# Second MLP of a two-block transformer kernel: unit 1 computed with seven block products instead of two plain columns, and the steps around it moved

## The chip, the core and the metric

One core of a Trainium2 chip runs the whole program. TensorE (PE in the profile) multiplies, ScalarE (ACT) and VectorE (DVE) prepare operands and take results out of the accumulators, GpSimd (POOL) and SyncE (SP) issue the DMAs. The metric is the device time of one execution in microseconds (us), as a median over runs.

## What is computed

Two blocks run one after the other on 256 tokens of width 2048. The change touches only the MLP at the end of the second block:

```python
h2 = rmsnorm(x, g_mlp[l])
u = jax.nn.relu(jnp.einsum('bsd,df->bsf', h2, w_up[l]))
x = x + jnp.einsum('bsf,fd->bsd', u * u, w_down[l])
...
return rmsnorm(x, g_final)
```

`w_up` is 2048 x 8192 and `w_down` 8192 x 2048, both float32: 64 MB each, read from HBM once.

## The kernel before

**Precision.** Every float32 operand is split into a high part and a low part (what the high part leaves). A product takes three matmuls: high x high, high x low of the weights, low x high. They are L626, L627 and L628 in plain products and L656, L657 and L658 (helper `three`) in the block products described below. ACT writes the high part of the weights into `w_high`, DVE then subtracts it from `raw` and writes `w_low`. In plain stretches these are L1154 and L1671, around block products and everything behind them L1283 and L1874. Both rings have four places (`LEAD = 4`). A filling of one place is called a *piece* here; `half_used` counts the pieces that PE has finished, and ACT may write piece n+4 only once PE is through with piece n.

**Units.** The hidden width is worked through in eight units of 1024. A unit has an up product (h2 by `w_up`, 16 pieces of plain work or 24 of block work), a squared ReLU, a redistribution, and a down product (16 pieces, `fast_down`) that adds to `xs`. A plain piece feeds 12 matmuls. A unit done with seven block products (`fast_up`) goes through four pairs of weight loads. Of the first load of a pair (`seven_products`) come pieces of 6, 6, 6 and 3 matmuls, of the second (`eight_products`) two pieces of 12: 45 matmuls a pair, 180 a unit. The seven products need sums of weight blocks, which DVE makes right behind the low part of a pair's first piece (`sum_weights`: L1888, L1891, L1893, all of which the second and third piece of the pair need), and sums of token blocks, called `combos`, made once for the whole MLP: eight DVE adds (`sum_tokens`, L1905 to L1913), one ACT copy (`split_combos`, L1294), one DVE subtraction (`low_combos`, L1918). The seven products that come out are put together by eight DVE adds (`combine`, L1926).

**The hidden half between up and down.** For every column of 512: ReLU on ACT (L1364 from PSUM behind plain work, L1311 behind block work), square on ACT (L1370 or L1316), block transposes on DVE (`turn_blocks`, L1988), sixteen DMAs that exchange 32-row blocks (from `blocks` in `scr` to `exchanged` in `extra`), high part on ACT (`take_exchanged`, L1225) and low part on DVE (`take_low`, L1865) into `u_high` and `u_low`. There is one `exchanged` buffer: the transposes of a column stand behind the take of the column before on DVE.

**Order.** Nothing schedules at run time. Each engine has a list written by hand, and semaphores tie the lists. In `first_eighths` ACT and DVE handle, at step y, piece y+4, and at the step after a plain column's last piece its ReLU, square and transposes; at y+6 its take. In the second MLP all of units 0 and 1 (four plain columns, `up_columns`) come first, then down 0, then `fast_up` of unit 2, down 1, and so on; `combos` are made around step 24 (`COMBOS_AT`). The sixteen DMAs of the four plain columns are issued by SP (`exchange_behind`, L435), among its weight loads; those of the other twelve columns by POOL (L565). In `fast_body` ACT and DVE take a unit in 40 steps (`STEP`: 24 up, 16 down), with combine at steps 21 to 23, ReLU and square at 23 and 25, transposes at 24 and 31, takes at 30 and 37 (`COMBINE_AT`, `RELU_AT`, `TURN_AT`, `TAKE_AT`), so that exchange and takes lie beside the down pieces.

## Time and profile before

| | us |
|---|---|
| median of 3 runs | 2055.24 (2051.26 to 2057.15) |
| time of the profiled execution | 2057.61 |
| its span, first to last instruction | 2055.8 |
| PE busy in the span | 1996.2 |
| DVE busy | 1545.9 |
| ACT busy | 1081.8 |
| POOL busy | 254.4 |
| second MLP, from its first matmul (1367.42) to the end of the span | 688.4 |

What lies outside the span is 2057.61 - 2055.8 = 1.8 us. A matmul's row shows how long one lasts (390 ns), but matmuls are pipelined: the distance of two starts is what one costs on the path, and it has to be read from a stretch.

### The profile page before, as it was taken

What the parts mean: (1) busy time and instruction counts of PE and PEld (TensorE: products, weight loads), DVE (VectorE), ACT (ScalarE), POOL (GpSimd) and SP (SyncE); (2) the same over time, 40 slices, a digit from 0 to 9 for tenths busy, and PEclk for the clock granted to TensorE, in tenths of its full rate; (3) what the DMA queues carried; (4) which work ended last, traced back from release to release, by engine and by line L of the source; (5) the groups of instructions that cost most, each with busy time, mean ns of one, the idle gap of its engine ahead of it and who ended that gap; (6) DMA issues with size and microseconds to landing.
All of it is one profiled execution on the core that took longest, in us unless ns stands there. A gap on an engine that the chain in (4) does not pass through costs nothing.

```text
span 2055.8 us, 23282 instructions
## 1 busy us (share of the span) xinstructions
PE 1996.2 (97%) x8761; PEld 1619.0 (79%) x8761; DVE 1545.9 (75%) x1644; ACT 1081.8 (53%) x1373; POOL 254.4 (12%) x505
## 2 busy tenths in 40 slices
PE   3999989999999999999999999999999999999998
PEld 1777568888788888887788888888888888888887
DVE  7989767767787988877556666756687887978875
ACT  3333526544545645555656755555455655655554
POOL 0000003001103021130002120000003113031130
PEclk9999999999999999999999999999999999999999
DMA  9999998879756666585556565456656667567573
GB/s 399 410 382 377 335 365 286 298 259 331 249 184 225 207 205 220 198 274 183 159 192 214 164 199 182 164 184 206 224 186 224 217 200 234 189 207 233 195 251 118
DMA packets 202523, 489.66 MB, mean 238 GB/s; under 512 B 18193, under 2 KB 24785, under 8 KB 193329
## 3 DMA queue, kind: packets, MB, share of 16 engines
q1 hardware_dynamic: 184784, 461.15, 65.1%
q0 software_dynamic: 16464, 23.62, 3.8%
q10 hardware_dynamic: 1168, 3.46, 0.4%
q8 instruction: 69, 1.13, 0.2%
q14 instruction: 38, 0.30, 0.0%
HBM read 461.94 MB, written 4.19 MB: 227 GB/s over the span
## 4 chain that ended last, share of the span: by engine, by line
PE 85%; DMA 6%; DVE 6%; ACT 2%; issue 0%; ACTq 0%; DVEq 0%
PE ps L626 21%; PE ps L627 21%; PE ps L628 21%; PE ps L657 7%; PE ps L656 7%; PE ps L658 7%; DVE scr L1684 2%; DMA raw<-in_w_mod 2%; DMA raw<-in_fnet_w 2%; DVE w_low L1671 2%; DMA raw<-in_w_mlp_in 2%; ACT w_high L1154 1%; PE ps L784 1%; DVE scr L1699 1%; PE ps L808 0%
## 5 line engine op out<-in xcount | busy, mean ns | idle before, releaser
L1283 ACT ACTIVATE w_high<-raw 128x1024 fp32r<-128x1024 f32 x392 | 414.5, 1060 | 399.9 <-PE ps L628 204.1
L1874 DVE TENSOR_TENSOR w_low<-raw,w_high 128x1024 fp32r<-128x1024 f32 x392 | 477.7, 1220 | 162.7 <-ACT w_high L1283 156.6
L1671 DVE TENSOR_TENSOR w_low<-raw,w_high 128x1024 fp32r<-128x1024 f32 x320 | 386.7, 1221 | 235.8 <-ACT w_high L1154 235.4
L1154 ACT ACTIVATE w_high<-raw 128x1024 fp32r<-128x1024 f32 x320 | 333.4, 1057 | 383.4 <-PE ps L628 260.6
L626 PE MATMUL ps<-w_high,u_high 128*128 128x512 f32 x1152 | 449.7, 390 | 0.7 <-DVE u_low L2281 0.7
L628 PE MATMUL ps<-w_high,u_low 128*128 128x512 f32 x1152 | 448.6, 389 | 0.0
L627 PE MATMUL ps<-w_low,u_high 128*128 128x512 f32 x1152 | 448.6, 389 | 0.0
L626 PE MATMUL ps<-w_high,h_both 128*128 128x512 f32 x896 | 358.1, 400 | 9.2 <-DVE w_low L1671 7.7
L627 PE MATMUL ps<-w_low,h_both 128*128 128x512 f32 x896 | 351.3, 392 | 0.0
L628 PE MATMUL ps<-w_high,h_both 128*128 128x512 f32 x896 | 351.2, 392 | 0.0
L565 POOL DMA_DIRECT2D extra<-scr x384 | 187.6, 497 | 1100.8 <-DVE scr L1988 978.4
L626 PEld LDWEIGHTS ps<-w_high,u_high 128*128 128x128 f32 x1152 | 216.4, 188 | 45.7 <-DVE u_low L2281 1.1
L628 PEld LDWEIGHTS ps<-w_high,u_low 128*128 128x128 f32 x1152 | 216.3, 188 | 45.1
L627 PEld LDWEIGHTS ps<-w_low,u_high 128*128 128x128 f32 x1152 | 216.4, 188 | 44.1
L626 PEld LDWEIGHTS ps<-w_high,h_both 128*128 128x128 f32 x896 | 169.8, 190 | 49.9 <-DVE w_low L1671 8.6
L628 PEld LDWEIGHTS ps<-w_high,h_both 128*128 128x128 f32 x896 | 169.6, 189 | 36.2
L627 PEld LDWEIGHTS ps<-w_low,h_both 128*128 128x128 f32 x896 | 170.0, 190 | 35.3 <-issue 1.4
L656 PE MATMUL ps<-w_high,h_both 128*128 128x512 f32 x440 | 171.3, 389 | 0.0
L658 PE MATMUL ps<-w_high,h_both 128*128 128x512 f32 x440 | 171.3, 389 | 0.0
L657 PE MATMUL ps<-w_low,h_both 128*128 128x512 f32 x440 | 171.3, 389 | 0.0
L1684 DVE SCALAR_TENSOR_TENSOR scr<-raw,silu_c,scr 128x2048 f32<-128x2048 f32 x64 | 150.4, 2350 | 10.4 <-DMA raw<-in_w_mod 5.3
L656 PEld LDWEIGHTS ps<-w_high,h_both 128*128 128x128 f32 x440 | 82.6, 188 | 17.3 <-DVE w_low L1874 0.2
(240 smaller groups left out, 1801.4 us busy)
## 6 DMA issues: line engine op xcount, KB each, us to landing
raw<-in_w_mod SPq DMA_DIRECT2D x96, 1024.0 KB, 7.5
raw<-in_w_mlp_in SPq DMA_DIRECT2D x64, 1024.0 KB, 5.7
raw<-in_w_mlp_out SPq DMA_DIRECT2D x64, 1024.0 KB, 5.3
raw<-in_w_up SPq DMA_DIRECT2D x64, 1024.0 KB, 5.2
raw<-in_w_down SPq DMA_DIRECT2D x64, 1024.0 KB, 5.2
raw<-in_w_in SPq DMA_DIRECT2D x48, 1024.0 KB, 5.2
raw<-in_fnet_w SPq DMA_DIRECT2D x16, 1024.0 KB, 7.0
raw<-in_w_out SPq DMA_DIRECT2D x16, 1024.0 KB, 5.1
```

Source lines behind the costliest of these rows:

```text
L565: eng.dma_start(exchanged[q * BLOCK:(q + 1) * BLOCK, a * RUN:(a + 1) * RUN], blocks[a * BLOCK:(a + 1) * BLOCK, q * RUN:(q + 1) * RUN])\
L626: eng.matmul(dst, ah, wh, start=(k == first), stop=False)
L627: eng.matmul(dst, ah, wl, start=False, stop=False)
L628: last = eng.matmul(dst, al, wh, start=False, stop=(k == end))
L656: eng.matmul(dst, a_high, wh, start=start, stop=False)
L657: eng.matmul(dst, a_high, wl, start=False, stop=False)
L658: return eng.matmul(dst, a_low, wh, start=False, stop=stop)
L1154: eng.activation(w_high[:, h % LEAD, :], raw[:, slot, (h % 2) * 2 * CW:(h % 2 + 1) * 2 * CW], ACT.Copy).then_inc(high_ready, 1)
L1283: eng.activation(ring(w_high, h % LEAD, 1 if part == 3 else 2), raw_blocks(slot, kind, part), ACT.Copy)\
L1671: eng.tensor_tensor(w_low[:, h % LEAD, :], raw[:, slot, piece], w_high[:, h % LEAD, :].bitcast(f32), ALU.subtract).then_inc(raw_used if h ...
L1684: eng.scalar_tensor_tensor(out=mod_acc(v), in0=raw[:, slot, :], scalar=silu_c[:, bass.ds(kk, 1)], in1=mod_acc(v), op0=ALU.mult, op1=ALU.ad ...
L1874: eng.tensor_tensor(ring(w_low, h % LEAD, count), raw_blocks(slot, kind, part), ring(w_high, h % LEAD, count).bitcast(f32), ALU.subtract). ...
```

## The change

The second MLP now has two plain columns (unit 0), then `fast_up` for units 1 to 7. `COMBOS_AT` goes from 24 to 8. For ACT and DVE `first_eighths` is replaced by `first_unit` (16 plain steps) and one `fast_body` over a single unit. In that body the steps that belong to the second plain column stand at fixed places: its square at step 0 (ACT), the take of column 0 and the transposes of column 1 at step 1, the take of column 1 at step 7. All 64 exchange DMAs that SP issued in this MLP are issued by POOL.

```diff
--- before.py
+++ after.py
@@ -141,7 +141,9 @@
 DOWN_BANKS = (4, 6, 0, 2)
 DOWN_ADDS = {4 * c + 3: c for c in range(NC)}
 FIRST_SLOTS = 4 * HALVES + DOWN_SLOTS
-FIRST_COMBOS_AT, COMBOS_AT = 36, 24
+FIRST_COMBOS_AT, COMBOS_AT = 36, 8
+PLAIN_UP = 2 * HALVES
+SQUARE_LATE, TURN_LATE, TAKE_LATE = 0, 1, 7
 ROWS_AT = 27
 COPY_AT = UNIT - 6
 COMBINE_AT = {UNIT - 3: 0, UNIT - 2: 1, UNIT - 1: 2}
@@ -514,13 +516,11 @@
                 chunk(w_out, j * 4 * P, c * CW)
                 exchange_qk_behind(12 * GROUPS + n)
 
-            for ch in range(4 * NC):
+            for ch in range(2 * NC):
                 mlp_chunk(w_up, w_down, 0, ch)
-                exchange_behind(ch)
-            for ch in range(2 * NC):
-                c, j = divmod(ch, 2)
-                chunk(w_down, j * 4 * P, c * CW)
-                exchange_behind(4 * NC + ch)
+            for m in range(HALVES):
+                up_chunk(w_up, 1, m)
+            down_chunks(w_down, 0)
             with t.loop(eng, 1, QUARTERS, raw=32) as q:
                 for part in range(2):
                     for m in range(HALVES):
@@ -591,11 +591,11 @@
                             eng.dma_start(mixed_exchanged[q * BLOCK:(q + 1) * BLOCK, a * RUN:(a + 1) * RUN],
                                           mixed_blocks[a * BLOCK:(a + 1) * BLOCK, q * RUN:(q + 1) * RUN])\
                                .then_inc(m_exchanged, 16)
-            for n in range((QUARTERS - 1) * NC):
-                if n == (QUARTERS - 1) * NC - 2:
-                    eng.wait_ge(combined, (4 + 6) * 8)
+            for n in range(QUARTERS * NC, 2 * QUARTERS * NC):
+                if n == 2 * QUARTERS * NC - 2:
+                    eng.wait_ge(combined, (4 + 7) * 8)
                     eng.dma_start(grow[:, :], g_final.broadcast_to([P, D])).then_inc(grow_in, 16)
-                exchange(n, (QUARTERS + 1) * NC + n + 1, range(QUADS))
+                exchange(n, n + 1, range(QUADS))
 
 
         @block.tensor
@@ -693,16 +693,19 @@
                                         k == 0 and n == tt == 1 and kk == 0, last and kk == 1)
                     ins.then_inc(half_used, 1)
 
-            def fast_up(pairs):
+            def fast_up(pairs, plain=False):
 
                 def before(n):
-                    if n in (0, 2):
+                    if plain and n in (0, 2):
+                        eng.wait_ge(up_taken, t.c["up"] - (n == 0))
+                    elif n in (0, 2):
                         eng.wait_ge(summed, t.c["summed"] - (n == 0))
 
                 for k in range(PAIRS):
                     seven_products(pairs, k, before if k == 0 else lambda n: None)
                     eight_products(k, before if k == 0 else lambda n: None)
                 t.add("combined", 8)
+                t.add("up", 2)
 
             def fast_down(e, plain=False, end=False, turn_behind=()):
 
@@ -837,8 +840,8 @@
             def h_ready(hh):
                 return t.c["stage"] + 1 + hh if hh % 2 == 0 else None
 
-            def up_columns(mods=(), turn_end=False):
-                for y, (c, hh) in enumerate(QUARTER_ORDER[:4 * HALVES]):
+            def up_columns(count, mods=(), turn_end=False):
+                for y, (c, hh) in enumerate(QUARTER_ORDER[:count * HALVES]):
                     if hh == 0 and c < 2:
                         eng.wait_ge(summed, t.c["summed"] + c - 1)
                     elif hh == 0:
@@ -852,7 +855,7 @@
                     if mods and y == ROWS_AT:
                         eng.wait_ge(raw_used, t.used())
                         sum_partitions_to_rows(G2)
-                t.add("up", NC)
+                t.add("up", count)
 
 
             eng.wait_ge(vec_in, 16 * 8)
@@ -964,7 +967,7 @@
                     eng.wait_ge(mod_cols, SC2B + 1)
                     idle_products(SUM_B_BANK, 4)
             t.add("t", 2 * NC)
-            up_columns(MOD_AFTER)
+            up_columns(NC, MOD_AFTER)
             eng.wait_ge(mod_cols, G2 + 1)
             fast_down(2, plain=True)
             eng.wait_ge(combos_low, 1)
@@ -1124,11 +1127,10 @@
                         eng.wait_ge(m_low, TT * GROUPS)
                     plain_turn(TT * j, TT * j + TT)
             t.add("stage", TT * NC)
-            up_columns(turn_end=True)
-            fast_down(0, plain=True)
+            up_columns(2, turn_end=True)
             eng.wait_ge(combos_low, 2)
-            for e in range(2, 2 * QUARTERS):
-                fast_up(combos)
+            for e in range(1, 2 * QUARTERS):
+                fast_up(combos, plain=e == 1)
                 fast_down(e - 1)
             fast_down(2 * QUARTERS - 1, end=True)
 
@@ -1315,21 +1317,52 @@
                 eng.wait_ge(up_taken, t.at("up", 0))
                 eng.activation(here, here, ACT.Square).then_inc(up_ready, 1)
 
-            def fast_body(behind, scaled):
-
-                slots = FAST_SLOTS + behind
-                for i in range(SLOTS_ALL):
+            def fast_body(behind, scaled, steps=(0, 1)):
+
+                slots = len(steps) * (FAST_UP + FAST_DOWN) + behind
+                for i in range(len(steps) * STEP):
                     fast_high(*slots[i + LEAD])
-                    step, j = divmod(i, STEP)
+                    n, j = divmod(i, STEP)
+                    step = steps[n]
+                    if len(steps) == 1 and i == SQUARE_LATE:
+                        eng.wait_ge(up_taken, t.c["up"])
+                        eng.activation(hidden, hidden, ACT.Square).then_inc(up_ready, 1)
+                    elif len(steps) == 1 and i in (TURN_LATE, TAKE_LATE):
+                        take_exchanged(int(i == TAKE_LATE), t.c["pool_moved"], pool=True)
                     if j == COPY_AT:
                         copy_first(i)
                     if j in RELU_AT:
                         relu_square(2 * step + RELU_AT[j], scaled)
                     if j in TAKE_AT:
                         take_exchanged(2 * step + TAKE_AT[j], t.at("pool_moved", 0), pool=True)
-                t.add("done", SLOTS_ALL)
+                t.add("done", len(steps) * STEP)
                 t.add("pool_moved", 4 * SHARE)
-                t.add("summed", 2 * NC)
+                t.add("summed", len(steps) * NC)
+
+            def first_unit(pairs, at, scaled):
+
+                for y in range(PLAIN_UP):
+                    if y + LEAD >= PLAIN_UP:
+                        fast_high(*FAST_UP[y + LEAD - PLAIN_UP])
+                    else:
+                        high_part()
+                    if y == at:
+                        split_combos(pairs)
+                    if y in UP_ENDS:
+                        eng.wait_ge(half_used, t.c["done"] + y + 1)
+                        t.add("up")
+                        eng.wait_ge(t_blocks, t.c["up"] - 1)
+                        if scaled:
+                            for tt in range(TT):
+                                last = eng.activation(hidden[:, tt, :], lin(UP_ENDS.index(y))[:, tt, :], ACT.Relu,
+                                                      scale=rstd[:, tt:tt + 1])
+                        else:
+                            last = eng.activation(hidden, lin(UP_ENDS.index(y)), ACT.Relu)
+                        last.then_inc(up_taken, 1)
+                        if y < PLAIN_UP - 1:
+                            eng.wait_ge(up_taken, t.c["up"])
+                            eng.activation(hidden, hidden, ACT.Square).then_inc(up_ready, 1)
+                t.add("done", PLAIN_UP)
 
             def last_down(target):
 
@@ -1632,7 +1665,8 @@
                 gain_turned(TT * (NC - 1) + tt, cols[:, V_GM:V_GM + KT])
             root()
             eng.wait_ge(rstd_ready, t.c["root"])
-            first_eighths(combos, COMBOS_AT, True)
+            first_unit(combos, COMBOS_AT, True)
+            fast_body(FAST_SLOTS, True, (1,))
             with t.loop(eng, 1, QUARTERS - 1, high=SLOTS_ALL, raw=32, pool_moved=4 * SHARE, done=SLOTS_ALL, up=NC,
                         summed=2 * NC, sums=6 * PAIRS, combined=16, copied=2):
                 fast_body(FAST_SLOTS, True)
@@ -1951,11 +1985,12 @@
                    .then_inc(summed, 1)
                 t.add("summed")
 
-            def fast_body(target, behind):
-
-                slots = FAST_SLOTS + behind
-                for i in range(SLOTS_ALL):
-                    step, j = divmod(i, STEP)
+            def fast_body(target, behind, steps=(0, 1)):
+
+                slots = len(steps) * (FAST_UP + FAST_DOWN) + behind
+                for i in range(len(steps) * STEP):
+                    n, j = divmod(i, STEP)
+                    step = steps[n]
                     if j - UNIT in DOWN_ADDS:
                         add_down(target, DOWN_ADDS[j - UNIT], i + 1)
                     if j in COMBINE_AT:
@@ -1965,7 +2000,11 @@
                         take_low(2 * step + TAKE_AT[j])
                     if j in TURN_AT:
                         turn_blocks((hidden, hidden_odd)[TURN_AT[j]])
-                t.add("done", SLOTS_ALL)
+                    if len(steps) == 1 and i in (TURN_LATE, TAKE_LATE):
+                        take_low(int(i == TAKE_LATE))
+                    if len(steps) == 1 and i == TURN_LATE:
+                        turn_blocks()
+                t.add("done", len(steps) * STEP)
 
             def last_down(target, after):
 
@@ -2007,6 +2046,21 @@
                     if y in FIRST_BLOCKS:
                         turn_blocks()
                 t.c["done"] = done + 64
+
+            def first_unit(pairs, at):
+
+                for y in range(PLAIN_UP):
+                    if y + LEAD >= PLAIN_UP:
+                        fast_low(*FAST_UP[y + LEAD - PLAIN_UP])
+                    else:
+                        low_part()
+                    if y == at - 4:
+                        sum_tokens()
+                    if y == at + 2:
+                        low_combos(pairs)
+                    if y == UP_ENDS[0]:
+                        turn_blocks()
+                t.add("done", PLAIN_UP)
 
             def first_eighths(target, pairs, at, mods=()):
 
@@ -2373,7 +2427,8 @@
                 gain_low(TT * (NC - 1) + tt, cols[:, V_GM:V_GM + KT])
             mean_square()
             invert()
-            first_eighths(xs, combos, COMBOS_AT)
+            first_unit(combos, COMBOS_AT)
+            fast_body(xs, FAST_SLOTS, (1,))
             with t.loop(eng, 1, QUARTERS - 1, low=SLOTS_ALL, raw=32, t=2 * NC, up=NC, done=SLOTS_ALL,
                         summed=2 * NC, sums=6 * PAIRS, combined=16, copied=2, first=12 * HALVES // 2):
                 fast_body(xs, FAST_SLOTS)
```

**DVE, behind the last plain column.** Before, the second unit was plain too, and its third and fourth column's steps stood among plain pieces and down pieces (L1671 is the low part of a plain or down piece, L1865 the take, L1988 the transposes, L1950 the sum of a down product, L1918 the low part of the combos):

```order
L1918 TENSOR_TENSOR combos<-scr,combos 128x2048
L1671 TENSOR_TENSOR w_low<-raw,w_high 128x1024 x3
L1865 TENSOR_TENSOR u_low<-extra,u_high 128x4x128 x2
L1671 TENSOR_TENSOR w_low<-raw,w_high 128x1024 x2
L1988 STREAM_TRANSPOSE scr<-scr 128x4x4x32 x2
L1671 TENSOR_TENSOR w_low<-raw,w_high 128x1024 x3
L1950 TENSOR_TENSOR xs<-ps,xs 128x2x512
```

Now (L1908 is the former L1874, L1922, L1925 and L1927 are the weight sums, L1899 the take, L2027 the transposes):

```order
L1908 TENSOR_TENSOR w_low<-extra,w_high 128x512
L1908 TENSOR_TENSOR w_low<-raw,w_high 128x1024 x2
L1899 TENSOR_TENSOR u_low<-extra,u_high 128x4x128 x2
L2027 STREAM_TRANSPOSE scr<-scr 128x4x4x32 x2
L1908 TENSOR_TENSOR w_low<-raw,w_high 128x1024
L1922 TENSOR_TENSOR raw<-raw 128x1024
L1925 TENSOR_TENSOR extra<-raw 128x512
L1927 TENSOR_TENSOR raw<-raw,extra 128x512
L1908 TENSOR_TENSOR w_low<-raw,w_high 128x1024 x2
L1908 TENSOR_TENSOR w_low<-extra,w_high 128x512
L1908 TENSOR_TENSOR w_low<-raw,w_high 128x1024 x2
L1899 TENSOR_TENSOR u_low<-extra,u_high 128x4x128 x2
```

The take of column 0 and the transposes of column 1 stand between the last piece of the first pair and the first piece of the second; the take of column 1 stands at the same place one pair later.

**ACT, same place.** Before (L1154 is the high part of a plain or down piece, L1364 ReLU, L1370 square, L1225 take, L1283 the high part of a block piece):

```order
L1225 ACTIVATE u_high<-extra 128x4x128 x2
L1154 ACTIVATE w_high<-raw 128x1024 x2
L1364 ACTIVATE scr<-ps,rstd 128x512 x2
L1370 ACTIVATE scr<-scr 128x1024
L1154 ACTIVATE w_high<-raw 128x1024 x6
L1225 ACTIVATE u_high<-extra 128x4x128 x2
L1154 ACTIVATE w_high<-raw 128x1024 x6
```

Now (L1285 is the former L1283, L1357 the ReLU of a plain column, L1329 the late square, L1227 the take):

```order
L1285 ACTIVATE w_high<-extra 128x512
L1357 ACTIVATE scr<-ps,rstd 128x512 x2
L1285 ACTIVATE w_high<-raw 128x1024
L1329 ACTIVATE scr<-scr 128x1024
L1285 ACTIVATE w_high<-raw 128x1024
L1227 ACTIVATE u_high<-extra 128x4x128 x2
L1285 ACTIVATE w_high<-raw 128x1024 x3
L1285 ACTIVATE w_high<-extra 128x512
L1285 ACTIVATE w_high<-raw 128x1024 x2
L1227 ACTIVATE u_high<-extra 128x4x128 x2
```

Both takes of unit 0 now stand within the first two pairs of a block unit, six pieces apart; before, the takes stood eight plain pieces apart.

## Rows read from the trace of the kernel before

**Rows 1.** Page, section 1: busy us, share of the span, instructions.
```profile
PE 1996.2 (97%) x8761; PEld 1619.0 (79%) x8761; DVE 1545.9 (75%) x1644; ACT 1081.8 (53%) x1373; POOL 254.4 (12%) x505
```

**Rows 2.** All waits of PE from 1300 us on: total, times, longest.
```profile
PE ps L626 <- DVE u_low L2281: 0.7, 1, 0.7
```

**Rows 3.** Windows plain up, down 0, block unit 2: PE, PEld, DVE, ACT, POOL busy; clock.
```profile
1367.42:1455.35 87.93, 87.93 (x394) 72.94 (x392) 56.55 (x65) 48.69 (x61) 0.00 (x0) 1.00 0.62 201
1455.35:1498.87 43.52, 43.52 (x194) 36.06 (x192) 27.92 (x26) 20.13 (x21) 0.00 (x0) 1.00 0.62 213
1498.87:1539.67 40.80, 40.80 (x182) 33.81 (x180) 36.79 (x38) 24.00 (x25) 0.00 (x0) 1.00 0.62 206
```

**Rows 4.** DVE timeline, second pair of block unit 2: start, us, idle before.
```profile
1501.52 3.95 DVE L1874 TENSOR_TENSOR w_low<-raw,w_high 128x1024 fp32r<-128x1024 f32 x3 [0.63 <-ACT w_high L1283]
1505.51 1.22 DVE L1888 TENSOR_TENSOR raw<-raw 128x1024 f32<-128x1024 f32 x1
...
1507.49 0.69 DVE L1893 TENSOR_TENSOR raw<-raw,extra 128x512 f32<-128x512 f32 x1
1508.10 2.44 DVE L1874 TENSOR_TENSOR w_low<-raw,w_high 128x1024 fp32r<-128x1024 f32 x2
```

**Rows 5.** PE timeline: starts of the second and third piece of that pair.
```profile
1510.43 0.39 PE L656 MATMUL ps<-w_high,combos 128*128 128x512 f32 x1
...
1511.79 0.39 PE L656 MATMUL ps<-w_high,h_both 128*128 128x512 f32 x1
```

**Rows 6.** Groups by line and form from 1300 us on: busy us, mean ns.
```profile
L1874 DVE TENSOR_TENSOR w_low<-raw,w_high 128x1024 fp32r<-128x1024 f32 x232 | 283.0, 1220 | 95.2 <-ACT w_high L1283 90.8
L1283 ACT ACTIVATE w_high<-raw 128x1024 fp32r<-128x1024 f32 x232 | 245.3, 1060 | 233.0 <-PE ps L628 116.1 <-DVE raw L1888 61.7 <-PE ps L658 48.1
...
L1283 ACT ACTIVATE w_high<-extra 128x512 fp32r<-128x512 f32 x24 | 15.1, 629 | 9.0 <-PE ps L628 9.0
```

**Rows 7.** ACT timeline: ReLU and square of the first plain column.
```profile
1391.24 1.25 ACT L1364 ACTIVATE scr<-ps,rstd 128x512 f32<-128x512 f32 x2
1392.52 1.06 ACT L1370 ACTIVATE scr<-scr 128x1024 f32<-128x1024 f32 x1
```

**Rows 8.** POOL and SP timelines: sixteen exchange DMAs of one column.
```profile
1394.94 10.71 SPq L435 DMA_DIRECT2D extra<-scr  x16
...
1633.40 7.81 POOL L565 DMA_DIRECT2D extra<-scr  x16 [59.38 <-issue]
```

**Rows 9.** DVE transposes and ACT takes of two columns in down stretches; first DVE take.
```profile
1629.84 1.30 DVE L1988 STREAM_TRANSPOSE scr<-scr 128x512 f32<-128x512 f32 x2
...
1645.07 1.15 ACT L1225 ACTIVATE u_high<-extra 128x512 fp32r<-128x512 f32 x2 [0.78 <-DMA extra<-scr]
1645.74 1.29 DVE L1865 TENSOR_TENSOR u_low<-extra,u_high 128x512 fp32r<-128x512 f32 x2 [0.19 <-ACT u_high L1225]
...
1967.18 1.30 DVE L1988 STREAM_TRANSPOSE scr<-scr 128x512 f32<-128x512 f32 x2
...
1982.14 1.15 ACT L1225 ACTIVATE u_high<-extra 128x512 fp32r<-128x512 f32 x2 [0.51 <-DMA extra<-scr]
```

**Rows 10.** Line L565 (POOL), then line L435 (SP): one exchange DMA to landing.
```profile
DMA to landing us min/median/max: 2.0/3.9/6.9
...
DMA to landing us min/median/max: 1.8/2.7/7.1
```

**Rows 11.** PE timeline, first block: two waits of PE; first and 14th matmul behind the second.
```profile
273.32 3.70 PE L767 MATMUL ps<-raw,silu_p 128*128 128x512 f32 x8 [2.99 <-DMA raw<-in_w_mod]
292.80 0.80 PE L626 MATMUL ps<-w_high,h_both 128*128 128x512 f32 x1 [3.19 <-DVE w_low L1671]
...
298.51 0.49 PE L627 MATMUL ps<-w_low,h_both 128*128 128x512 f32 x1
```

**Rows 12.** Windows, PE: busy us (matmuls), then granted clock, behind each of the two waits.
```profile
274.00:276.00 2.00, 2.00 (x6) 1.00 0.99 371
...
294.00:296.00 2.00, 2.00 (x7) 0.50 1.01 370
```

## What the change will do to the time, predicted before it ran

> **What bounds the kernel now.** The page's busy table comes first. PE is busy for 97% of the span, DVE for 75% and ACT for 53% [rows 1]. A busy PE need not be a PE without holes, so the waits come second: from 1300 us on, which takes in the whole second MLP, PE waits for anything only once, 0.7 us, and that is before this MLP [rows 2]. The windows show the same by stage: every stretch is filled to its end, at full granted clock [rows 3]. So this MLP's time is the number of its matmuls times their distance. Down 0 has 16 pieces of 12, 192 matmuls in 43.52 us: 0.2267 us each. Block unit 2 has 180 in 40.80 us: again 0.2267. The 390 ns of a matmul's own row would give nearly twice what one costs here.
>
> The third view asks how much room there is beside PE, since the change moves other engines' work into a block unit. In block unit 2 DVE is busy for 36.8 of 40.8 us, in the plain stretch for 56.6 of 87.9, in down 0 for 27.9 of 43.5 [rows 3]. A block unit is thus nearly as much DVE's as PE's, on average; its pairs have to be looked at singly. In the second pair of unit 2 DVE ends the first piece's low part at 1505.5, makes the three weight sums from 1505.51 to 1508.2, and only then the low parts of the second and third piece: 1508.10 to 1510.54 for both, 1509.3 for the second [rows 4]. PE starts the second piece at 1510.43 and the third at 1511.79 [rows 5]. The slack is 1.1 to 1.3 us. Whatever is put ahead of this chain on DVE beyond that, PE waits for.
>
> **What the change takes away.** Unit 1 goes from 192 matmuls of plain work to 180: 12 x 0.2267 = 2.72 us less, all of it on the path, as PE has no holes here. SP loses 64 exchange DMAs (10.7 us for each column, during which no load can be issued [rows 8]); PE and the converters never waited for these loads [rows 2], so that gives nothing. The down products, the final stage and the six later block units are as before.
>
> **What moves without cost.** The token sums and combos come 16 steps earlier. DVE's part is eight adds of 512 columns, at the 0.69 of the 512-wide weight sums [rows 4] 5.5 us, and a subtraction of 2048 columns, twice a low part, 2.4; ACT's is a copy of 2048 columns, twice a high part, 2.1 [rows 6]. They go into plain pieces, which leave DVE 1.5 us of every 2.72 (a low part is 1.22 [rows 6]), with the ring's four pieces, 10.9 us, as a buffer: the low part held up by the token sums comes out some 2 us ahead of its piece. Cover: the ring's lead. If it failed, the loss would be at most the 5.5 us of the sums. I take nothing.
>
> **What the first pair of unit 1 costs.** Let 0 be the end of the last plain piece. PE's pieces are then 1.36, 1.36, 1.36, 0.68, 2.72, 2.72 long, so the first pair lasts to 10.20, and the second pair's second piece is due at 11.56. ACT may write the piece four ahead once PE is through with one; rows stand for each step, and back to back both engines gain about 0.08 an instruction.
> - ACT: fourth piece 0.2 to 0.85 (0.63 [rows 6]); ReLU of column 1 to 2.05 (1.25 [rows 7]); fifth piece to 3.1; square to 4.1; sixth piece to 5.1; take of column 0 to 6.2 (1.14); seventh piece to 7.2. PE needs this ReLU at 3.4, in the middle of its third piece, when it starts on the bank that column 1 used: covered, with 1.3 to spare.
> - DVE: low part of the sixth piece 5.1 to 6.3; low take of column 0 to 7.6 (1.29 [rows 9]); transposes of column 1 to 8.85 (1.30 [rows 9]); low part of the seventh piece to 10.1, just in time; the three sums to 12.8 (2.67 [rows 4]); low part of the eighth to 13.95.
>
> PE wants the eighth at 11.56 and starts it about 0.1 behind the low part: **it waits 2.5 us**. Behind that the ring is short but holds: the remaining pieces of the pair come out before PE asks.
>
> **What the second pair costs.** The take of column 1 stands after the high part of the 12th piece. ACT is there at about 16.7. The blocks must have been exchanged by then. From the end of the transposes, an exchange is a start of some 0.3, sixteen issues in 7.81 [rows 8] and the last landing, 2.0 to 6.9 with 3.9 in the middle [rows 10]: 12.0 in sum. Whole exchanges that a take had to wait for are a direct reading: 1645.07 - (1629.84 + 1.30) = 13.9 and 1982.14 - (1967.18 + 1.30) = 13.7 [rows 9]; the first began late on POOL, at 1633.40 [rows 8], the second had a slow landing. I take 12.9, between the sum and these two. The take then starts at 8.85 + 12.9 = 21.75, and ACT stands still for five microseconds with nothing that it could pass. Behind it: take to 22.9, high part of the 13th piece to 23.9; DVE low take to 24.3, low part of the 13th to 25.5. PE, late by 2.5, wants that piece at 20.4 + 2.5 = 22.9: **it waits 2.7 us**. The 13th is the first of a pair, so the sums follow at once, 25.5 to 28.2, and the low part of the 14th to 29.4. PE wants it at 25.6 + 1.36 = 27.0 and **waits 2.5 us** again. Afterwards the distances are those of an ordinary block unit, which PE runs without waiting.
>
> **The sum.** -2.72 + 2.5 + 2.7 + 2.5 = +5.0 us. The profiled execution goes from 2057.61 to 2062.6. Against the median of 2055.24 it gives 2060.2, or 0.24% more. Ends: with the fastest landing (0.3 + 7.81 + 2.0 = 10.1) the take starts at 18.95 and the middle wait vanishes, +2.3; with the slowest (15.0) it is 4.8, +7.1.
>
> **Two rules weighed.** Sixteen exchange DMAs took SP 10.7 us and POOL 7.8 [rows 8], with a middle landing of 2.7 and 3.9 [rows 10]: from first issue to last landing 13.4 against 11.7. The Trainium skill's page "DMA: Bandwidth & Descriptors", section "Issuing engine by pattern", calls the SP and ACT path generally faster, and its specifications put the first byte 0.4 us earlier on it. By the page the move to POOL would add an estimated 0.4 us to the middle wait, +5.4 in all; by the rows it shortens the exchange, and the sum stays.
>
> In the window of down 0, with POOL idle, and over all 232 low parts, of which many lay beside POOL's issues, DVE's low part keeps its 1220 ns [rows 6]. The skill's page "GPSIMD Engine Reference", section 8 "Key points", says that GpSimd contends with VectorE instructions that read two SBUF inputs, which these do; by it the moved issues would slow the low parts. The 1220 ns don't bear that out, and no term is made of it.
>
> **Rivals.** *The clock falls (slower still).* PE waits three times within 20 us, the last two with only 1.36 us of matmuls between them. A single wait of 2.99 us between dense matmuls left the clock at 1.00, the upper level (2.4 GHz); one of 3.19 us behind a run of very small matmuls ended with 0.50, the lower level (1.2 GHz) [rows 11, 12]. There 13 matmuls took 298.51 - 292.80 = 5.71 us where 13 x 0.2267 is 2.95: 2.8 us lost per fall. For it: two waits so near each other; against it: the 2.99 us that did no harm. 2060.2 + 2.8 = 2063.0. The skill's page "TensorE: Matmul & The Clock Gate", "Key points", warns that idle gaps between bursts of matmuls bring the clock down to half; here one gap did and one didn't.
>
> *The exchange is in time.* If column 1's blocks were there when ACT comes (16.7 - 8.85 = 7.8 us after the transposes), the last two waits would vanish, since the take then costs 1.14 and 1.29 us in a place with that much room: -2.72 + 2.5 = -0.2, or 2055.0. Against it: POOL alone needs 7.81 us to issue.
>
> *The block unit absorbs everything (faster).* The mechanism is the one DVE chain of the second pair. If DVE has at least 2.5 us more room than I read there (say ACT and DVE run further ahead than the ring's count of four lets me believe) and the exchange comes early as well, only the matmuls count: 2055.24 - 2.72 = 2052.5. It decides at DVE ready for the seventh piece before 6.4 instead of 8.85. Against it are the 1.1 us of slack measured in a pair without any inserted work [rows 4, 5].
>
> **How the numbers follow.** Forecast (three waits, clock kept) 0.55; clock falls 0.22; exchange in time 0.10; everything absorbed 0.08; a debt of DVE that is carried into further pairs, above 2066, 0.05. The likeliest case is 2060.2, by its ends 2057.5 to 2062.3. The range leaves out the top and the bottom tail: 2053.5 to 2066. A measurement of this kernel can tell about 0.3%, 6.2 us, from no change. Slower by more takes 2061.4: most of the clock case, and about a quarter of the forecast's own spread, 0.34. Faster by more needs 2049.1, for which no case has the matmuls, 0.02. Within: 0.64.
>
> **What would show it.** In the changed kernel's trace: 12 matmuls fewer; a block unit 1 that lasts 48 to 49 us instead of 40.8; PE waits on the line that writes low parts, 2.4 to 2.6 us each, at the 8th and 14th piece of that unit, and one of 1 to 4 us at the 13th; ACT idle for about 5 us before the second take, released by a DMA; granted clock 1.00 throughout, or 0.50 behind the third wait in the rival. Units 2 to 7 still take 40.8 and 43.5. I would be wrong if PE waits for nothing in unit 1, or if the wait at the 8th piece is there without DVE's take and transposes ahead of it.

## The result, and the profile after

| | before | changed |
|---|---|---|
| median | 2053.74 us | 2059.56 us |
| lowest and highest of 14 runs | 2050.74, 2058.66 | 2055.48, 2062.20 |
| span of the profiled execution | 2055.8 | 2059.9 |
| matmuls | 8761 | 8749 |
| unit 1's up product, in the trace | plain, 43.5 | 49.4 |

The ratio is 1.0026, interval 1.0018 to 1.0035: slower by 5.3 us (3.7 to 7.2). That is clear of noise but below 0.3%. The prediction was 2060.2, +5.0 on the median it was given.

The busy table of the changed kernel answers [rows 1]: 12 matmuls fewer, and 64 more instructions on POOL.

```profile
PE 1996.4 (97%) x8749; PEld 1616.5 (78%) x8749; DVE 1566.7 (76%) x1672; ACT 1088.2 (53%) x1382; POOL 285.7 (14%) x569
```

The waits of PE from 1300 us on (total, times, longest) answer [rows 2]. The 0.7 us ahead of this MLP is there as before, the first line is new:

```profile
PE ps L656 <- DVE w_low L1908: 5.3, 3, 1.9
PE ps L626 <- DVE u_low L2335: 0.7, 1, 0.7
```

The windows answer [rows 3]: unit 1's up product, down 0, unit 2's up product.

```profile
1410.05:1459.45 49.40, 44.08 (x182) 35.13 (x180) 38.93 (x42) 27.30 (x32) 7.81 (x16) 0.93 0.53 181
1459.45:1502.97 43.52, 43.52 (x194) 36.04 (x192) 32.78 (x36) 23.53 (x26) 15.62 (x32) 1.00 0.67 218
1502.97:1543.77 40.80, 40.80 (x182) 33.78 (x180) 37.31 (x39) 24.00 (x25) 0.00 (x0) 1.00 0.59 206
```

The whole loss is in the first line: 49.40 us for work that takes 40.80 in unit 2, and a mean granted clock of 0.93. The two stretches behind it last what they lasted before. In the PE timeline of that window the three waits stand at the 8th, the 13th and the 14th piece (start, duration, idle before):

```profile
1423.58 0.50 PE L656 MATMUL ps<-w_high,combos 128*128 128x512 f32 x1 [1.81 <-DVE w_low L1908]
...
1434.65 0.50 PE L656 MATMUL ps<-w_high,h_both 128*128 128x512 f32 x1 [1.92 <-DVE w_low L1908]
...
1438.50 0.79 PE L656 MATMUL ps<-w_high,combos 128*128 128x512 f32 x1 [1.59 <-DVE w_low L1908]
...
1442.43 0.40 PE L656 MATMUL ps<-w_high,combos 128*128 128x512 f32 x1
```

The idle time in brackets is less than what a wait costs, since it counts from a matmul's end, and a matmul lasts 0.39 us where its neighbours start 0.23 apart. The distances of the starts give the cost. In front of the 8th piece, the last start before the wait is at 1421.38, so the next was due at 1421.61: 1.97 us, and 0.11 more because the first matmul behind a wait is followed after 0.34. That makes 2.1. The 13th piece was due at 1432.58 and came at 1434.65: 2.2 with the same addition. The 14th was due at 1436.13 at full clock and came at 1438.50: 2.4. (Counted from that place, it holds the 0.4 us that the lower clock took from the end of the 13th piece.) Behind it nine matmuls took 3.93 us (1438.50 to 1442.43) where 2.04 would do: 1.9. Sum 8.6, the excess of the window. Less the 2.7 of the twelve matmuls it is +5.9, and so much longer is the whole stretch: from the MLP's first matmul to the end of the span it is 688.4 us before and 2059.9 - 1365.6 = 694.3 now.

ACT's and DVE's timelines show both causes. First the DVE chain in front of the 8th piece:

```profile
1416.08 1.29 DVE L1899 TENSOR_TENSOR u_low<-extra,u_high 128x512 fp32r<-128x512 f32 x2
1417.28 1.30 DVE L2027 STREAM_TRANSPOSE scr<-scr 128x512 f32<-128x512 f32 x2
1418.50 1.18 DVE L1908 TENSOR_TENSOR w_low<-raw,w_high 128x1024 fp32r<-128x1024 f32 x1
1419.72 1.22 DVE L1922 TENSOR_TENSOR raw<-raw 128x1024 f32<-128x1024 f32 x1
...
1422.31 2.49 DVE L1908 TENSOR_TENSOR w_low<-raw,w_high 128x1024 fp32r<-128x1024 f32 x2
```

Then POOL's sixteen issues, and ACT standing in front of the take:

```profile
1418.88 7.81 POOL L565 DMA_DIRECT2D extra<-scr  x16 [17.64 <-DVE scr L2027]
...
1431.24 1.16 ACT L1227 ACTIVATE u_high<-extra 128x512 fp32r<-128x512 f32 x2 [4.91 <-DMA extra<-scr]
```

From the end of the transposes (1418.58) to the take it is 12.7 us, where the prediction took 12.9.

And the windows behind the second and third wait (PE busy, then granted clock):

```profile
1435.00:1436.00 1.00, 1.00 (x5) 0.75 0.00 0
1436.00:1437.00 1.00, 0.92 (x3) 0.50 0.00 0
...
1441.00:1442.00 1.00, 1.00 (x4) 0.50 0.47 39
1442.00:1443.00 1.00, 1.00 (x5) 0.84 0.89 297
```

The clock is at its lower level (1.2 GHz) from about 1435.5 to 1442.3.

### The profile page after: what moved, and what is told of

It is laid out like the page before. It is cut to its first block, busy times and chain, and to the rows that moved or that the text cites. A ratio compares the mean times of both kernels' runs of the same rounds, so it can differ in the third digit from the quotient of the medians.

```text
span 2059.9 us, 23304 instructions
## 1 busy us (share of the span) xinstructions
PE 1996.4 (97%) x8749; PEld 1616.5 (78%) x8749; DVE 1566.7 (76%) x1672; ACT 1088.2 (53%) x1382; POOL 285.7 (14%) x569
## 4 chain that ended last, share of the span: by engine, by line
PE 84%; DMA 7%; DVE 7%; ACT 2%; issue 1%; POOL 0%; ACTq 0%; DVEq 0%
PE ps L626 20%; PE ps L627 20%; PE ps L628 20%; PE ps L656 7%; PE ps L657 7%; PE ps L658 7%; DVE scr L1718 2%; DMA raw<-in_w_mod 2%; DMA raw<-in_fnet_w 2%; DVE w_low L1705 2%; DMA raw<-in_w_mlp_in 2%; DVE scr L1733 1%; ACT w_high L1156 1%; PE ps L787 1%; POOL extra L565 0%
## 5 line engine op out<-in xcount | busy, mean ns | idle before, releaser
L1285 ACT ACTIVATE w_high<-raw 128x1024 fp32r<-128x1024 f32 x428 | 452.2, 1059 | 433.3 <-PE ps L628 217.7
L1908 DVE TENSOR_TENSOR w_low<-raw,w_high 128x1024 fp32r<-128x1024 f32 x428 | 521.0, 1220 | 174.6 <-ACT w_high L1285 168.4
L565 POOL DMA_DIRECT2D extra<-scr x448 | 218.9, 497 | 1076.7 <-DVE scr L2027 969.6
L626 PE MATMUL ps<-w_high,h_both 128*128 128x512 f32 x832 | 332.7, 400 | 8.2 <-DVE w_low L1705 6.4
L628 PE MATMUL ps<-w_high,h_both 128*128 128x512 f32 x832 | 326.0, 392 | 0.0
L627 PE MATMUL ps<-w_low,h_both 128*128 128x512 f32 x832 | 326.0, 392 | 0.0
L626 PEld LDWEIGHTS ps<-w_high,h_both 128*128 128x128 f32 x832 | 157.5, 189 | 47.2 <-DVE w_low L1705 7.6
L656 PE MATMUL ps<-w_high,h_both 128*128 128x512 f32 x484 | 188.9, 390 | 1.9 <-DVE w_low L1908 1.9
L657 PE MATMUL ps<-w_low,h_both 128*128 128x512 f32 x484 | 188.8, 390 | 0.0
L658 PE MATMUL ps<-w_high,h_both 128*128 128x512 f32 x484 | 188.7, 390 | 0.0
L628 PEld LDWEIGHTS ps<-w_high,h_both 128*128 128x128 f32 x832 | 157.4, 189 | 33.6
L627 PEld LDWEIGHTS ps<-w_low,h_both 128*128 128x128 f32 x832 | 157.7, 190 | 32.9 <-issue 1.4
L656 PEld LDWEIGHTS ps<-w_high,h_both 128*128 128x128 f32 x484 | 91.0, 188 | 21.4 <-DVE w_low L1908 2.5
```

What stands on the lines that cost most here:

```text
L565: eng.dma_start(exchanged[q * BLOCK:(q + 1) * BLOCK, a * RUN:(a + 1) * RUN], blocks[a * BLOCK:(a + 1) * BLOCK, q * RUN:(q + 1) * RUN])\
L626: eng.matmul(dst, ah, wh, start=(k == first), stop=False)
L627: eng.matmul(dst, ah, wl, start=False, stop=False)
L628: last = eng.matmul(dst, al, wh, start=False, stop=(k == end))
L656: eng.matmul(dst, a_high, wh, start=start, stop=False)
L657: eng.matmul(dst, a_high, wl, start=False, stop=False)
```

## The experiments

A difference of a microsecond is hard to see in the time of the whole: in the thirteen traces this MLP starts anywhere from 1361.4 to 1368.7 us, though nothing ahead of it was touched. The length of unit 1's up product is the same for one program and one course of the clock to within 0.05 us, so it carries the verdicts, and the ratios stand beside it.

**The take one pair later.** Does the late exchange cost the second and third wait?

```diff
-SQUARE_LATE, TURN_LATE, TAKE_LATE = 0, 1, 7
+SQUARE_LATE, TURN_LATE, TAKE_LATE = 0, 1, 13
```

> The changed kernel with one number changed: the take of column 1 stands at step 13 of unit 1 instead of 7 (one pair later). Theory A (two DVE chains and one late exchange): the exchange needs 12.7 us behind the transposes and has landed by then, so the waits of PE at the 13th and 14th piece of unit 1 and the fall of the clock behind them go; the wait of about 2.0 us at the 8th piece stays. Unit 1 lasts 40.8 + 2.1 = 42.9 us (49.4 in the changed kernel), and the whole is 2.7 - 2.1 = 0.6 us faster than the kernel before. Rival B (the move of the exchanges from SP to POOL, or the block unit's added DVE work as such, costs the time): unit 1 stays near 49 us or the loss turns up elsewhere, and the kernel stays 5 us slower than before. Rival C (the granted clock alone): the waits stay and only 1.9 us come back.

Measured: only one wait is left, the one at the 8th piece. Ratio to before 0.9986 (0.9977 to 0.9995). PE timeline, and the windows of unit 1 and of a stretch in it (us, busy by engine, clock):

```profile
1421.54 0.58 PE L656 MATMUL ps<-w_high,combos 128*128 128x512 f32 x1 [1.81 <-DVE w_low L1908]
...
1408.01:1452.58 44.57, 42.76 (x181) 34.77 (x180) 38.78 (x42) 27.22 (x32) 7.81 (x16) 0.96 0.59 200
...
1422.00:1424.00 2.00, 2.00 (x6) 1.57 (x5) 2.00 (x3) 0.97 (x2) 2.00 (x5) 0.50 0.25 66
```

Unit 1 is 44.57 us instead of 49.40. It is not the expected 42.9, since here the clock fell behind the first wait. That I had not reckoned with. The second and third wait belong to the exchange alone, as theory A has it: the take, with the same work, stands at the same place of the next pair and costs nothing there. Rival B, that the moved work as such costs the time, is out, and so is rival C. The ratio is lower than the window can explain: 44.57 - 40.80 - 2.72 = +1.0 us by the window, -2.9 by the ratio (-4.7 to -1.0). I have no cause for that difference. Two more executions of the same program (e8_take13_2 and e9_take13_3, below) took 2054.03 and 2056.12 us beside one of 2052.91 of the kernel before; single executions lie some 4 us to either side of the median, so this settles nothing.

**The take of column 0 out of the chain.** As before, and the take of column 0 into a plain step:

```diff
+TAKE_FIRST = 14
...
+                    if y == TAKE_FIRST:
+                        take_exchanged(0, t.c["pool_moved"], pool=True)
...
+                    if y == TAKE_FIRST:
+                        take_low(0)
```

> As e1_take13, and the take of column 0 (ACT 1.14 us, DVE 1.29 us) moved out of step 1 of unit 1 into step 14 of the plain columns. Theory A: the DVE chain in front of the 8th piece becomes 1.2 us shorter and the wait falls from 2.0 to about 0.9 us; unit 1 lasts 41.8 us, the whole is 1.7 us faster than before. Rival B: no difference to e1_take13, since the amount of work is the same.

Measured: one wait, and unit 1 of 41.79 us. Ratio 0.9996 (0.9987 to 1.0005). PE timeline:

```profile
1425.45 0.50 PE L657 MATMUL ps<-w_high,combos 128*128 128x512 f32 x1 [0.59 <-DVE w_low L1911]
```

The wait costs 0.9 by the distances, from 2.1: the 1.2 us of DVE's low take, all of it on the path. No fall of the clock. By the window this version is at 41.79 - 40.80 - 2.72 = -1.7 us against the kernel before, which lies in the interval of the ratio (-2.7 to +1.0).

**All four steps where DVE has room.**

```diff
-SQUARE_LATE, TURN_LATE, TAKE_LATE = 0, 1, 7
+SQUARE_LATE, TURN_LATE, TAKE_LATE = 1, 6, 17
+TAKE_FIRST = 14
```

> All four steps moved to where DVE has room: take of column 0 at plain step 14, square of column 1 at step 1, its transposes at step 6, its take at step 17 of unit 1. Theory A: no wait of PE in unit 1, which lasts 40.8 us; only the 12 matmuls count, 2.7 us (0.13%) faster than the kernel before and about 8 us faster than the changed kernel. Rival B: slower than before by several us still.

Measured: 2050.94 us against 2053.87, ratio 0.9988 (0.9979 to 0.9997), -2.5 us where the matmuls alone give -2.7. No wait of PE. Windows of unit 1 and of down 0:

```profile
1409.74:1450.56 40.82, 40.82 (x181) 33.80 (x180) 38.14 (x42) 26.48 (x30) 7.81 (x16) 1.00 0.65 219
1450.56:1494.08 43.52, 43.52 (x193) 36.05 (x192) 32.88 (x36) 23.53 (x26) 15.63 (x32) 1.00 0.67 218
```

DVE is busy for 38.14 us here and 38.93 in the changed kernel: the work is nearly the same, only its places differ. This version beats both kernels, the kernel before by little (the interval is -4.3 to -0.6 us).

**POOL instead of SP, alone.** The kernel before, with its four plain columns, and only the issuer changed:

```diff
-                exchange_behind(ch)
...
-            for n in range((QUARTERS - 1) * NC):
+            for n in range(QUARTERS * NC, 2 * QUARTERS * NC):
...
-                exchange(n, (QUARTERS + 1) * NC + n + 1, range(QUADS))
+                exchange(n, n + 1, range(QUADS))
```

> The kernel before with one part of the change alone: the 64 exchange DMAs of the four plain columns of the second MLP are issued by POOL instead of SP. Theory A: no effect, as neither PE nor the converters waited for SP's loads; PE waits for nothing in this MLP, the four plain columns last 87.9 us as before, ratio 1.000. By the rule that the SP path is the faster one the takes would come later; at their old places they have 12.7 us, so PE would still not wait. Rival B (the move to POOL costs time): several us slower.

Measured: ratio 1.0002 (0.9993 to 1.0011), no wait of PE in the MLP, block unit 2 of 40.80 us. Once ACT had to wait for a take, which PE did not feel; POOL had begun late:

```profile
1436.09 7.83 POOL L563 DMA_DIRECT2D extra<-scr  x16 [16.23 <-issue]
...
ACT u_high L1223 <- DMA extra<-scr: 2.2, 1, 2.2
```

The transposes had ended at 1433.83, 2.3 us before. This was no chance. In all thirteen traces the third and the ninth sequence that POOL issues in this MLP begin 2.3 and 3.0 us behind the end of their transposes, and nearly all others 0.3, whichever column the sequence carries. In the trace of the changed kernel the third carries the first column of unit 1 (DVE, then POOL):

```profile
1465.35 1.30 DVE L2027 STREAM_TRANSPOSE scr<-scr 128x512 f32<-128x512 f32 x2
...
1468.91 7.81 POOL L565 DMA_DIRECT2D extra<-scr  x16 [42.22 <-issue]
```

The late start goes with the place in POOL's list; why, no run shows. The sequence of column 1 of unit 0, on which the second wait hangs, is the second of that list and began 0.3 us behind. At the third place it would have lengthened the wait by 2 us.

**DVE's time, without the moved steps.** On the arrangement that has no wait, two or three additions whose result nobody reads, at step 1, ahead of the seventh piece:

```diff
+                    if len(steps) == 1 and i == 1:
+                        for _ in range(2):
+                            link(eng.tensor_tensor(qk_moved[:, :], xs[:, 0, 0:2 * CW], xs[:, 1, 0:2 * CW], ALU.add))
```

> The arrangement of e3_best, which has no wait in unit 1, with two extra DVE additions of 1024 columns (their result is used nowhere) at step 1, ahead of the first piece of the second pair: about 2.5 us of DVE work where the changed kernel has its take and transposes. Theory A: DVE has 1.1 us of room there, so PE waits about 1.4 us at the 8th piece and nowhere else but for 0.2 at the 14th; unit 1 lasts 42.3 us without a fall of the clock. Rival (it is the take or the transposes as such, not DVE's time): no wait.

> As e6_extra2 with three extra additions, 3.8 us. Theory A: the wait at the 8th piece grows by one addition, to about 2.6 us; unit 1 lasts 43.5 us without a fall of the granted clock and up to 1.9 us more with one. A single wait of 1.8 us was followed by a fall in e1_take13, one of 0.6 us in e2_take0_early was not: I expect a fall behind this one.

Measured: unit 1 of 42.42 us with two and 43.68 with three. The PE timelines, two first:

```profile
1418.73 0.50 PE L657 MATMUL ps<-w_high,combos 128*128 128x512 f32 x1 [1.16 <-DVE w_low L1911]
...
1422.40 0.50 PE L657 MATMUL ps<-w_high,combos 128*128 128x512 f32 x1 [2.19 <-DVE w_low L1911]
```

By the distances the wait is 1.4 us, then 2.5. An addition more makes unit 1 1.26 us longer, 1.1 of it in this wait and 0.2 at the piece before, so it is paid one for one, and 2.5 us of work less a wait of 1.4 leaves the 1.1 us of room that [rows 4, 5] had shown. It is DVE's time that counts, whatever it is spent on. Three additions did not bring the clock down, against my expectation.

**The exchange's part alone.** As with the take of column 0 moved out, and the take of column 1 back at step 7:

> As e2_take0_early, but with the take of column 1 back at step 7: the exchange's part without most of the first wait. Theory A: wait of about 0.9 us at the 8th piece, then 2.1 and 2.4 us at the 13th and 14th, since the take still starts 12.7 us behind the transposes however late PE is; unit 1 lasts 40.8 + 5.5 = 46.3 us, with a fall of the clock up to 1.9 more. Rival (the second and third wait come from DVE's debt out of the first pair): they shrink with the first.

Measured: ratio 1.0017 (1.0008 to 1.0026), unit 1 of 46.57 us. PE timeline, and ACT's in front of the take:

```profile
1421.16 0.50 PE L657 MATMUL ps<-w_high,combos 128*128 128x512 f32 x1 [0.59 <-DVE w_low L1911]
...
1432.39 0.80 PE L657 MATMUL ps<-w_high,h_both 128*128 128x512 f32 x1 [2.10 <-DVE w_low L1911]
...
1436.23 0.50 PE L657 MATMUL ps<-w_high,combos 128*128 128x512 f32 x1 [0.92 <-DVE w_low L1911]
...
1428.97 1.15 ACT L1228 ACTIVATE u_high<-extra 128x512 fp32r<-128x512 f32 x2 [5.07 <-DMA extra<-scr]
```

The first wait is small and the second is as large as ever (2.3), so it is no debt out of the first pair. The transposes ended at 1416.15: 12.8 us to the take. The clock fell during the second wait; PE then took 0.43 us a matmul for the 13th piece, while DVE was still busy with the sums, and the third wait shrank to 1.3, counted from the last start before it. Counted from where the 14th piece was due at full clock, as the 2.4 of the changed kernel is, it is 2.5: the waits of 0.9, 2.3 and 2.5 then make up 5.7 of the 5.8 us that this unit is over 40.80. The fall cost next to nothing here, as the wait that followed hid it.

**The same programs again, for the clock.**

> The changed kernel once more, for a second profile of it beside the others. Theory A: waits of 2.0, 2.0 and 1.6 to 2.4 us at the 8th, 13th and 14th piece of unit 1 again; whether the granted clock falls to 0.50 behind the second of them may differ from execution to execution. If it falls, unit 1 lasts some 49.4 us, if not, some 47.5.

> The kernel of e1_take13 once more, for the granted clock alone. Its PE wait of 1.8 us at the 8th piece was followed by 1.7 us of work at the lower level in one profile. If the fall belongs to the program, unit 1 lasts 44.6 us again; if it differs from execution to execution, it may be 42.9 us with the clock at 1.00 throughout.

> As e8_take13_2, a third profile of the same program: unit 1 of 44.6 us with a fall, of 42.9 us without.

> The changed kernel, a third profile. The waits at the 8th, 13th and 14th piece again; unit 1 lasts 47.5 us if the clock keeps its upper level, 48 to 49.4 us if it falls behind the first or the second wait, as in its two profiles so far.

Measured, with the window of unit 1 in each profile (the third waits of the first profile and of e10_after_3 are counted from where the piece was due at full clock, all others from the start before):

| program | profile | waits (cost, us) | lower level | unit 1, us |
|---|---|---|---|---|
| changed | first | 2.1, 2.2, 2.4 | behind the 2nd | 49.40 |
| changed | e5_after_again | 2.1, 0.9, 2.5 | behind the 1st | 47.98 |
| changed | e10_after_3 | 2.1, 2.1, 2.4 | behind the 2nd | 49.39 |
| take at 13 | e1_take13 | 2.1 | behind the 1st | 44.57 |
| take at 13 | e8_take13_2 | 2.1 | none | 43.00 |
| take at 13 | e9_take13_3 | 2.1 | behind the 1st | 44.61 |
| take at 7, column 0 early | e7_take7_only | 0.9, 2.3, 1.3 | in the 2nd | 46.57 |
| three additions | e6_extra3 | 2.5 | none | 43.68 |
| two additions | e6_extra2 | 1.4 | none | 42.42 |
| column 0 early | e2_take0_early | 0.9 | none | 41.79 |

One program, the take at 13, has both outcomes, so the fall is not the program's alone. The windows of unit 1 in e8_take13_2 and e9_take13_3 (the clock is the first number behind the busy times):

```profile
1408.72:1451.72 43.00, 41.19 (x181) 33.63 (x180) 38.70 (x42) 27.22 (x32) 7.84 (x16) 1.00 0.60 208
...
1409.20:1453.81 44.61, 42.79 (x181) 34.77 (x180) 38.73 (x42) 27.32 (x32) 7.84 (x16) 0.96 0.59 200
```

It costs 1.6 us there (44.6 against 43.0). In e5_after_again it cost about as much behind the first wait, but the second wait shrank with it from 2.2 to 0.9, as PE came later to a piece whose time was set by the exchange:

```profile
1423.30 0.50 PE L656 MATMUL ps<-w_high,combos 128*128 128x512 f32 x1 [1.82 <-DVE w_low L1908]
...
1434.69 0.50 PE L656 MATMUL ps<-w_high,h_both 128*128 128x512 f32 x1 [0.65 <-DVE w_low L1908]
...
1438.54 0.50 PE L656 MATMUL ps<-w_high,combos 128*128 128x512 f32 x1 [2.19 <-DVE w_low L1908]
```

e5_after_again was also timed: ratio 1.0030 (1.0017 to 1.0042), the first comparison over again.

## Why the prediction was right, point by point

**Twelve matmuls, 2.72 us.** Right: e3_best, with nothing else left over, is 2.5 us faster (0.6 to 4.3).

**Combos and SP's exchanges at nothing.** Right. The plain stretch has no wait in any of the traces, and POOL in SP's place alone changed nothing (1.0002). [rows 2] list PE's waits alone and do not show that the converters never waited for a load; the trace before has no such wait of ACT in this MLP.

**First wait, 2.5 predicted, 2.1 measured.** The mechanism is shown by e2_take0_early and the two runs with additions. The term was too large because DVE got through its chain sooner: it began the low take 6.03 us after the unit's start and not at 6.3, and back to back the take, the transposes and the low part begin 1.20 and 1.22 apart where I had counted 1.3 and 1.25. The transposes ended at 8.53 and not at 8.85, and the 8th piece started at 13.53 and not at 14.05.

**Second and third wait, 2.7 and 2.5 predicted, 2.2 and 2.4 measured.** Shown by e1_take13 (gone with a later take) and e7_take7_only (there without the first). The exchange took 12.7 us against 12.9, and as the transposes were over sooner too, the take began at 21.2 us of the unit and not at 21.75. In the four traces in which ACT stood for this exchange it took 12.6 to 13.0. The nearness of 12.7 to 12.9 is in part luck: both of the whole exchanges that I had for a reading, 13.9 and 13.7, had something that this one had not, a start 2.3 us late or a slow landing.

**The two rules weighed.** Neither showed. The exchange by POOL took 12.6 to 13.0 us where the rows had given 12.9 and the first rule 0.4 more. The low parts of DVE were not slower beside POOL's issues: the pair at 1422.31, with POOL issuing, took 2.49 us, and so did the same pair of the next load, with POOL idle:

```profile
1437.23 2.49 DVE L1908 TENSOR_TENSOR w_low<-raw,w_high 128x1024 fp32r<-128x1024 f32 x2
```

**The clock.** Here the working was wrong. The forecast kept the clock and the fall was a rival with 0.22; it fell in all three profiles of the changed kernel. The step that failed is the reading of [rows 11, 12]: from one wait of 2.99 us that did no harm I took it that shorter ones are mostly harmless. A first wait of 2.1 us was followed by the fall in three profiles of six. A second one of 2.1 to 2.3 us with the clock still up went with a fall in all three profiles that have one (in e7_take7_only before the wait was over), and one of 2.5 us in neither of two (e6_extra3, and the third of e5_after_again). The Trainium skill's page "TensorE: Matmul & The Clock Gate", section "Why this matters for your kernels" (the prediction calls the section "Key points"), warns of idle gaps between bursts of matmuls; the traces agree for some of the waits and not for others of the same length. The price was too high as well: 1.6 to 1.9 us where I had 2.8, and less where a later wait hides it.

**The sum.** +5.0 was waits of 7.7 less 2.7. The first profile has waits of 6.7, a fall of 1.9, less 2.7: +5.9; the second profile, 47.98 - 43.52, has +4.5. The ratio says +5.3. So the time came out close partly by luck, because two errors, waits 1.0 us too large and a fall of 1.9 left out, went against each other. Unit 1 lasted 49.4, 48.0 and 49.4 us where 48 to 49 were forecast, and the wait at the 8th piece was 2.1 where 2.4 to 2.6 were. The case "exchange in time" and the case "everything absorbed" are out as forecasts of this placement, though e3_best shows that the block unit does absorb all four steps at other places.

## What to carry to other kernels

An average busy share (DVE 90% of a block unit) does not say where work may be put: look for the tightest chain, read the slack there from two rows, and price an inserted instruction one for one beyond it. A step that waits for a transfer belongs where the transfer is over by the rows, counted from its trigger, since an in-order engine that stands for it holds back everything listed behind. Saved matmuls are worth their start-to-start distance, here 0.227 us and not 0.39. Twelve of them gained 2.7 us here, and steps at the wrong places lost 8.6.

## What the runs showed of the hardware

A wait of TensorE of some 2 us between dense matmuls can be followed by a stretch at the lower clock level, and the same program shows it in one execution and not in another. The stretch held 5 to 9 matmuls whose rows last 0.63 us, 0.42 or 0.43 from start to start where 0.23 is usual; where its cost can be read apart from a later wait it is 1.6 to 1.9 us, and next to nothing in e7_take7_only, where a wait followed at once. In this MLP no wait of 1.4 us or less was followed by one.

An exchange of sixteen small DMAs by POOL had landed 12.6 to 13.0 us after its trigger in the four traces of the changed order in which ACT waited for it. The third and the ninth of POOL's sequences in this MLP began 2.3 and 3.0 us behind a trigger that had already come, in all thirteen traces, and the others mostly 0.3. The late starts go with the place in POOL's list and not with what the sequence carries; the traces show no reason for them.
